# A two-block transformer step on one core: stream updates in chunks between weight granules, feature rounds two ahead of their reader, later square sums

## What is computed

```python
for layer in range(DEPTH):
    i = layer // 2
    u = rms_norm(h, mix_norm_pre[layer])
    ...
    h = h + rms_norm(u, mix_norm_post[layer])
    u = swiglu(rms_norm(h, ffn_norm_pre[layer]), ffn_w_gate[layer], ffn_w_up[layer], ffn_w_down[layer])
    h = h + rms_norm(u, ffn_norm_post[layer])
```

## Time and profile before

| what | value |
|---|---|
| time, median of 3 runs | 3060.84 us (3059.07 to 3060.97) |
| the profiled execution: its span, first to last instruction | 3056.1 us (the page has no other time of it) |
| TensorE busy | 2929.4 us, 96% |
| VectorE busy | 1733.2 us, 57% |
| ScalarE busy | 1417.3 us, 46% |
| mean granted TensorE clock | 0.986 |
| DMA | 515 MB, 169 GB/s |

### The profile page before, as it was taken

How to read it: one execution, slowest core, us unless ns; L and a number is a source line. 1 busy time by engine, 2 the same in 40 slices (tenths; PEclk the granted TensorE clock), 3 DMA queues, 4 the chain that set the end, 5 groups by cost and what they waited for, 6 DMA issues and landing times.

```text
span 3056.1 us, 34851 instructions
## 1 busy us (share of the span) xinstructions
PE 2929.4 (96%) x13709; PEld 2409.1 (79%) x13709; DVE 1733.2 (57%) x2222; ACT 1417.3 (46%) x1809; POOL 74.0 (2%) x66
## 2 busy tenths in 40 slices
PE   8999999999999999999999999999999998888998
PEld 7878878788888888878877788888888876656776
DVE  5775655544544454554445544544445569988545
ACT  5543375544444444454446544444444454343444
POOL 0000000000000000000000000000000021210000
PEclk9999999999999999999999999999999999989999
DMA  6532235555555555555552555555555553324543
GB/s 232 176 125 93 87 138 196 179 191 185 190 193 193 193 180 192 193 178 186 187 178 97 181 198 189 182 193 192 193 192 192 181 176 112 97 91 159 179 154 124
DMA packets 255293, 515.45 MB, mean 169 GB/s; under 512 B 8240, under 2 KB 8464, under 8 KB 254144
## 3 DMA queue, kind: packets, MB, share of 16 engines
q1 hardware_dynamic: 252896, 501.61, 48.4%
q0 software_dynamic: 2272, 12.10, 1.1%
HBM read 511.58 MB, written 2.10 MB: 168 GB/s over the span
## 4 chain that ended last, share of the span: by engine, by line
PE 86%; DVE 9%; ACT 3%; issue 2%; DMA 0%; SPq 0%; DVEq 0%; ACTq 0%
PE acc L464 79%; PE side L655 2%; DVE u L1606 2%; DVE u L2207 1%; DVE pc L1606 1%; DVE wlo L1618 1%; ACT ar L1006 1%; DVE ar L1606 1%; PE side L521 1%; DVE ar L1609 1%; PE side L766 1%; ACT whi L1017 1%; PE side L550 1%; ACT xh L1006 0%; ACT L1006 0%
## 5 line engine op out<-in xcount | busy, mean ns | idle before, releaser
L1618 DVE TENSOR_TENSOR wlo<-raw,whi 128x1024 fp32r<-128x1024 f32 x948 | 1156.4, 1226 | 1124.0 <-ACT whi L1017 1123.1
L1017 ACT ACTIVATE whi<-raw 128x1024 fp32r<-128x1024 f32 x948 | 997.9, 1060 | 1232.0 <-PE acc L464 1230.8
L464 PE MATMUL acc<-whi,xh 128*128 128x512 f32 x3072 | 1220.6, 397 | 55.6 <-DVE wlo L1618 49.3
L464 PE MATMUL acc<-whi,xl 128*128 128x512 f32 x3072 | 1204.4, 392 | 0.0
L464 PE MATMUL acc<-wlo,xh 128*128 128x512 f32 x3072 | 1204.1, 392 | 0.0
L464 PEld LDWEIGHTS acc<-whi,xh 128*128 128x128 f32 x3072 | 582.2, 190 | 187.6 <-DVE wlo L1618 37.3
L464 PEld LDWEIGHTS acc<-whi,xl 128*128 128x128 f32 x3072 | 581.5, 189 | 123.5
L464 PEld LDWEIGHTS acc<-wlo,xh 128*128 128x128 f32 x3072 | 582.5, 190 | 117.1
L464 PE MATMUL acc<-whi,hTh 128*128 128x512 f32 x720 | 281.1, 390 | 2.7 <-ACT u L1006 2.7
L464 PE MATMUL acc<-wlo,hTh 128*128 128x512 f32 x720 | 280.8, 390 | 0.0
L464 PE MATMUL acc<-whi,hTl 128*128 128x512 f32 x720 | 280.8, 390 | 0.0
(11 more groups left out here) (227 smaller groups left out, 1345.2 us busy)
## 6 DMA issues: line engine op xcount, KB each, us to landing
raw<-in_ffn_w_gate SPq DMA_DIRECT2D x88, 1024.0 KB, 5.0
raw<-in_ffn_w_up SPq DMA_DIRECT2D x88, 1024.0 KB, 5.0
raw<-in_ffn_w_down SPq DMA_DIRECT2D x88, 1024.0 KB, 5.0
raw<-in_ev_w_in SPq DMA_DIRECT2D x56, 1024.0 KB, 4.9
raw<-in_od_w_in SPq DMA_DIRECT2D x48, 1024.0 KB, 5.1
raw<-in_w_in SPq DMA_DIRECT2D x32, 1024.0 KB, 5.4
raw<-in_ev_w_out SPq DMA_DIRECT2D x16, 1024.0 KB, 5.0
raw<-in_od_w_out SPq DMA_DIRECT2D x16, 1024.0 KB, 5.0
```

Source lines behind the costliest of these rows:

```text
L464: mm = pe.matmul(acc[2 * pair + t][:], x[:, k0 + j, tok], w[:, ring, j], start=first and j == 0 and n == 0, stop=last and j == 1 and n == 2)
L1017: act.activation(whi[:, place % RING], raw_granule(place), ACT.Copy).then_inc(S("hi_done"), 1)
L1618: dve.tensor_tensor(wlo[:, place % RING], raw_granule(place), whi[:, place % RING].bitcast(F32), ALU.subtract).then_inc(S("lo_done"), 1)
```

## The change

- TensorE (`features_use`): rounds 0 and 1 ahead of granule 0, then one round ahead of each of granules 1 to 6 (round j+1 ahead of granule j).
- ScalarE and VectorE: `lead` has `features_hi`/`features_lo` of rounds 0 and 1 alone (`AHEAD`); rounds 2, 3, 4, 5 come after splits 3, 4, 5, 6, rounds 6 and 7 after split 7 (`ROUNDS_AT`).
- VectorE at the four boundaries (`into_stream`, `rest`): of the last chunk's two products by the gain one comes before the reduction and one after the features of rounds 0 and 1. Chunk 0 of `h` is updated ahead of these features, chunk 1 behind that second product, chunk 2 after split 3, chunk 3 after split 5.
- `STATS` goes from 5 to 8: the squares come after split 8, the reciprocal after split 9.

```diff
-STATS = 5
+AHEAD = 2
+ROUNDS_AT = {3: (2,), 4: (3,), 5: (4,), 6: (5,), 7: (6, 7)}
+STATS = 8
...
                     if c == 0:
-                        if src is not None and j < 3:
-                            to_features(name, src, (range(4), range(4, 6), range(6, 8))[j])
+                        if src is not None and j < 7:
+                            to_features(name, src, range(AHEAD) if j == 0 else (j + 1,))
                         wait_features(name, j + 1)
...
+        STAGED = ("ev_out", "od_in", "od_out", "s_in", "s_out")
...
+                        if name in STAGED and c == 0 and j in ROUNDS_AT:
+                            features_hi(name, ROUNDS_AT[j])
...
-                features_hi("ev_out")
+                features_hi("ev_out", range(AHEAD))
...
-                            if first and m == 0 and j == STATS and name[3] == "a":
+                            if first and m == 0 and j in ROUNDS_AT and name[3] == "a":
+                                features_hi(name, ROUNDS_AT[j])
+                            if first and 8 * m + j == STATS and name[3] == "a":
                                 stats(NORM[name], h, JUNK)
...
+                        if name in STAGED and c == 0 and j in ROUNDS_AT:
+                            rest(name, j)
...
-            def gained(name, c):
+            def gained(name, c, tiles=range(TT)):
...
-                for t in range(TT):
+                for t in tiles:
                     dve.wait_ge(S("sq_done"), 8 * n + 2 * c + t + 1)
...
+            def stream_chunk(n, c):
+
+                if c == 3:
+                    dve.wait_ge(S("ug_done"), 8 * n + 8)
+                for t in range(TT):
+                    cl = slice(c * CH, c * CH + CH)
+                    stt(h[:, t, cl], u[:, t, cl], rstd_u[:, t:t + 1], h[:, t, cl], ALU.mult, ALU.add, "h_done")
+
             def into_stream(name, user):
 
                 n = POST[name]
+                gained(name, 3, (0,))
                 dve.wait_ge(S("sq_done"), 8 * n + 8)
...
-                dve.wait_ge(S("ug_done"), 8 * n + 8)
+                dve.wait_ge(S("ug_done"), 8 * n + 6)
                 if n == 0:
                     dve.wait_ge(S("x_back"), 16)
-                for c in range(4):
-                    for t in range(TT):
-                        cl = slice(c * CH, c * CH + CH)
-                        stt(h[:, t, cl], u[:, t, cl], rstd_u[:, t:t + 1], h[:, t, cl], ALU.mult, ALU.add, "h_done")
-                    if c:
-                        features_lo(user, range(2 * c - 2, 2 * c))
-                features_lo(user, range(6, 8))
+                stream_chunk(n, 0)
+                features_lo(user, range(AHEAD))
+                gained(name, 3, (1,))
+                stream_chunk(n, 1)
+
+            FROM = {"up0a": "ev_out", "od_in": "dn0b", "up1a": "od_out", "s_in": "dn1b"}
+
+            def rest(user, j):
+
+                if user in FROM and j in (3, 5):
+                    stream_chunk(POST[FROM[user]], 2 if j == 3 else 3)
+                features_lo(user, ROUNDS_AT[j])
```

More of the change, by code:

```diff
@@ L1079, in features_hi @@
                 base = 8 * TOF[name]
-                if name != "ev_gdn":
+                if name != "ev_gdn" and 0 in rounds:
                     act.wait_ge(S("used"), GRAN0["ple" if name == "pg" else name])
@@ L1377, in lead @@
                     rms_out(before)
-                    features_hi(f"up{l}a")
+                    features_hi(f"up{l}a", range(AHEAD))
                 hidden(f"up{l}a", lead)
@@ L1391, in lead @@
                 rms_out("dn0b")
-                features_hi("od_in")
+                features_hi("od_in", range(AHEAD))
             def od_aside(c, j):
-                if (c, j) == (0, STATS):
+                if 8 * c + j == STATS:
                     stats(NORM["od_in"], h, JUNK)
@@ L1435, in lead @@
                 attention()
-                features_hi("od_out")
+                features_hi("od_out", range(AHEAD))
             linear("od_out", lambda c: square_out("od_out", c), lead)
@@ L1445, in lead @@
                 rms_out("dn1b")
-                features_hi("s_in")
+                features_hi("s_in", range(AHEAD))
             def turned_wide(n, ready, done, outs):
@@ L1535, in lead @@
                 glu_out(3)
-                features_hi("s_out")
+                features_hi("s_out", range(AHEAD))
             def s_out_aside(c, j):
@@ L1933, in gained @@
                 cl = slice(c * CH, c * CH + CH)
-                if name[:2] == "dn":
+                if name[:2] == "dn" and 0 in tiles:
                     l = int(name[2])
@@ L1997, in block_of @@
                                     hidden_product(i + (n0 - 1))
-                            if first and m == 0 and j == STATS + 1 and name[3] == "a":
+                            if first and m == 0 and j in ROUNDS_AT and name[3] == "a":
+                                rest(name, j)
+                            if first and 8 * m + j == STATS + 1 and name[3] == "a":
                                 reciprocal_rms(NORM[name])
@@ L2017, in lead @@
                 def lead():
-                    gained(before, 3)
                     into_stream(before, f"up{l}a")
@@ L2029, in lead @@
             def lead():
-                gained("dn0b", 3)
                 into_stream("dn0b", "od_in")
             linear("od_in", lambda c: None, lead,
-                   lambda c, j: reciprocal_rms(NORM["od_in"]) if (c, j) == (0, STATS + 1) else None)
+                   lambda c, j: reciprocal_rms(NORM["od_in"]) if 8 * c + j == STATS + 1 else None)
             def attention():
@@ L2063, in attention @@
                         recip(n - 1)
-            linear("od_out", lambda c: gained("od_out", c), lambda: (attention(), features_lo("od_out")))
+            linear("od_out", lambda c: gained("od_out", c), lambda: (attention(), features_lo("od_out", range(AHEAD))))
             feed_forward(1, "od_out")
             def lead():
-                gained("dn1b", 3)
                 into_stream("dn1b", "s_in")
@@ L2363, in s_out_aside @@
                            hTh[:, 0:2, t * P:t * P + P].bitcast(F32), ALU.subtract, "pl_done")
-            linear("s_out", s_out, lambda: (pool_gate(3), glu_out(3), features_lo("s_out")), s_out_aside)
+            linear("s_out", s_out, lambda: (pool_gate(3), glu_out(3), features_lo("s_out", range(AHEAD))), s_out_aside)
             for c in range(4):
```

2 lines of the change are left out of this document (1 added, 1 removed).

## The result

| | before | changed |
|---|---|---|
| median of 20 runs each | 3060.06 us | 3064.26 us |
| lowest to highest | 3057.68 to 3062.42 | 3061.80 to 3066.40 |
| span of the profiled execution | 3056.1 us | 3062.3 us |
| mean granted clock of TensorE | 0.986 | 0.984 |

The ratio is 1.0013, with a 95% interval from 1.0007 to 1.0019: 2.1 to 5.8 us slower, 4.2 us by the medians. The forecast was +4.5 us.

A forecast was written before the change was run, and what follows sets the result against it. TensorE, busy 96% of the span, was the bound: only its idle stretches or clock could give time. Terms -2.4 - 0.8 - 0.6 + 1.05 + 5.1 + 0.45 + 1.7 gave +4.5 us, 3065.3 us; range 3057.5 to 3069.0.

The forecast's parts named there:

- (a): Four boundaries: one product by the gain less ahead of the sums, everything after comes 0.6 us earlier: -2.4 us.
- (e): Clock at the boundaries: the 1.0 us pause adds a 3.4 us low piece at three of four: +5.1 us.
- (g): In front of `s_out`: the pause grows to 3.4 us and the clock falls behind it: +1.7 us.
- (b): Granule 0 at four boundaries: waits for two rounds, not four, starting 0.2 us sooner at each: -0.8 us.
- (c): Granules 0 to 8 at four boundaries: moved transposes take almost all of the `wlo` wait saved: -0.6 us.
- (d): Granule 9 at three boundaries: late by 0.35 us because the next norm's squares move to granule 8: +1.05 us.
- the second rival: At `od_in` and `s_in`: the low clock goes on for a third piece; +7.9 us, 3068.7 us; chance 15%.
- (f): At `ev_out`, `od_out`, `s_out`: transposes moved behind granule 0 cost 0.15 us each: +0.45 us.
- The first rival: At the boundaries and `s_out`: the pauses leave the clock alone; -2.3 us, 3058.5 us; chance 27%.
- The last one: At the boundaries: shorter first idle stretches mean the clock never falls; -10.1 us, 3050.7 us; a rival with chance 6%.

The follow-up runs named there:

- e2_product: The kernel before with only one of the last chunk's two products by the gain moved behind the first features: 3057.84 us, ratio 0.9991.
- the filler: The changed kernel with four unread identity transposes in the pause before granule 0 at the four boundaries: 3060.01 us; again 3060.90 us.
- e8_split_squares: The changed kernel with the next norm's squares cut in two, one token tile after split 8, the other after split 9: 3066.81 us, single run.
- the third group: Repeat runs on a third chip of the changed kernel and three others, beside the kernel before (3060.25 us); the changed kernel took 3064.59 us.
- e6_warm_after: The changed kernel with 30 unread transposes in the first wait for `h` at the four boundaries: 3056.31 us, ratio 0.9988.

## Why the prediction held, term by term

The number (3065.3 forecast, 3064.26 measured; +4.5 and +4.2 us) rests on three large terms. Of these one was right, (a); one had the right mechanism and reached its size partly by luck, (e); and one was too big, (g).

- **(a) One product less, -2.4 us.** Right: `e2_product` alone gave 2.6, and the wait for `h` was 0.60 or 0.61 us shorter at each boundary.
- **(b) and (e), granule 0 and the clock, -0.8 and +5.1 us.** The two can't be told apart in one trace, since a clock that falls later speeds the transposes and slows the granules. Together they made +5.5 us at the four boundaries: 4.67 in the table, with 2.4 of (a) added and 1.5 of (c) and (d) taken off. The forecast had 4.3. The pause of 1.0 us (1.25 at `s_in`) stood where it was said to, and the low time grew by three times 3.4 us, as forecast. That the count agrees is luck. The forecast had the pause act at three boundaries; it acts at all four. What hid one of them is where the clock fell: TensorE resumed 0.88 us or more after the fall at two boundaries in the profile before (`od_in`, `s_in`) and at one in the changed kernel's (`up1a`), so four additions less one came to three. Their places are not those of the forecast: none at `od_in` and `s_in`, one at `up0a`, two at `up1a`. A low stretch of 10.2 us was the second rival's case (15%). It does occur, at four of 16 boundaries with the pause (in the second profile at `up1a` and `s_in`), but it goes with a late resumption and not with a particular boundary. The price of one addition was set too high: the filler removed three of them and gave back 3.7 us by the medians, an estimated 1.2 each and not 1.7. Part of the longer low stretch is the pause itself, in which there is no work to slow. By the rule of the Trainium skill weighed there (TensorE: Matmul & The Clock Gate, Part 4: PE-mode transpose) four transposes in the pause would have been no work for the clock. The runs speak against it: four more shortened the low time from 30.7 and 34.1 us to 20.5, and 30 more kept the clock full. This holds for these float32 transposes of 128x128, the only ones tried.
- **(c) Transposes moved, -0.6 us.** Mis-sized. At full clock granules 0 to 8 take 24.80 us, against 24.73 before, so the term is +0.3: the `wlo` waits went as said, and the 24 transposes between granules cost about 0.2 us more in each product than six times 0.45 us.
- **(d) Granule 9 late, +1.05 us.** Right: 0.41 to 0.43 us in three products (+1.25), nothing in `s_in`, and `e8_split_squares` names the cause. The profile shows only 0.10 us of it as a wait in front of granule 9, since the matmuls before it end late; it is the starts that are 0.4 us apart. ScalarE's chain ran as counted, with no drain behind a table load: in `up0a` the load at 614.64 took 1.28 us, and the next instruction began at 615.94. The Trainium skill's 1.38 us (ScalarE: Activation LUTs, What ACT_TABLE_LOAD costs) isn't seen here either.
- **(f) The three other products, +0.45 us.** Too small: 0.37 us each, 1.1 in all, for the reason given at (c).
- **(g) A low stretch in `s_out`, +1.7 us.** This step failed in size. I took one row, 3.47 us of idleness with a fall behind it, for a rule. The pause was forecast well (3.38 us), and in the profiled execution the fall came; but in four of six profiles it didn't. On average it is worth about a third of 1.7, some 0.6 us; one profile can't tell it.

With these sizes the sum is -2.4 + 5.5 + 0.3 + 1.25 + 1.1 + 0.6 = +6.35 us, from a few profiles; the medians say +4.2, and with the third group's +4.3. Most of the 2 us between them come from the pair of executions that was profiled: they lie 6.2 us apart, since that of the kernel before was 2.2 us faster than its median. Which term that makes too large isn't shown. For the same reason the prediction misread the distance between its span (3056.1) and its median (3060.8): around the span stand only 1.8 us, the other 2.9 are the fast execution. The forecast doesn't suffer by it, since the sum was added to the median.

The first rival (the pauses leave the clock alone) is refuted by the table of low times. The last one (the clock never falls) was wrong in its condition: the first idle stretches of 3.8 and 4.4 us are not short enough, and it takes work in them. Its size was too large as well: it stood 14.6 us below the forecast, and `e6_warm_after` lies 7 to 8 us below the changed kernel.

What was not tried: the idle stretches of the state-space part, behind which the clock is low for 44 to 51 us. By my reading of the kernel no accumulator bank is free there for unread transposes.

## What to carry to other kernels

A short pause is not priced by its length alone. Look at the clock around it: pauses of 1.0 to 1.5 us at four places cost about 4 us together where they fell inside a low stretch, and nothing for the clock where it was full, so keep TensorE dense behind each long wait, even with work that nobody reads. And to begin a product sooner with fewer features pays only if the features were what the first granule waited for: here the chain transpose, high half, low half of the first round bound it, and the transposes that had filled that wait for free came back later at full price, 0.98 us a product.

And a single profile is one draw of the clock. Here the same order had low stretches of 3.4 or 6.8 us, depending on when the clock fell; sort the stretches by that before you count what a change did.

## What the runs showed of the hardware

- The low stretches at the boundaries were 3.4, 6.8 or 10.2 us long, in those of 10.2 us with 6.8 to 8.1 us of work inside. Without a pause they were 3.4 us where TensorE resumed at most 0.7 us after the fall of the clock (14 of 14), and 6.8 us where it resumed 0.88 us or more after it (12 of 12). A pause of 0.57 to 1.47 us shortly after resuming added 3.4 us in all 18 cases.
- Transposes alone hold TensorE's clock. With 30 in a wait of 3.8 or 4.4 us, of which 0.3 and 1.16 us stayed idle, it was full throughout, and a pause of 1.47 us, only 1.1 us after the idle 1.16 us, left it full.
- Idleness of the same length does and doesn't bring the clock down: 2.51 us once in eight profiles, 3.38 us twice in six.
- Adding 30 transposes at each of four places took 4.6 us off the kernel's time; they lie wholly within a wait.
